# Cache attention of a decoder step: the rotary half of the scores moved from TensorE to GpSimd and VectorE

## The reference, cut to what matters

```python
def mla_keys(ckv, kpe, w_uk, g_kn):
    k_nope = jnp.einsum('btc,chd->bthd', ckv, w_uk)           # 256 latents -> 8 heads x 64
    k_pe = jnp.broadcast_to(kpe[:, :, None, :], k_nope.shape[:3] + (QK_ROPE_DIM,))   # 32, shared by the heads
    return rms_norm(jnp.concatenate([k_nope, k_pe], axis=-1), qk_gain(g_kn))

def update(carry, ckv_blk, kpe_blk, mask):                    # for every page of the cache
    k = mla_keys(ckv_blk, kpe_blk, w_uk, g_kn)
    s = jnp.einsum('bqhd,bkhd->bhqk', qf, k) * scale
    ...
```

## Time and profile before

| | |
|---|---|
| median of 3 runs | 2243.34 us (2241.21 to 2244.95) |
| span of the profiled execution | 2241.9 us; its time outside the span is not recorded, the median of the runs is 1.4 us above the span |
| cache attention within it | about 412 to 1338 us, eight sequences, 116.3 us from one tail to the next |
| TensorE busy | 2191.6 us (98%) |
| VectorE busy | 1425.7 us (64%) |
| ScalarE busy | 955.5 us (43%) |
| GpSimd busy | 363.4 us (16%) |
| granted TensorE clock, mean | 0.994 |

### The profile page before, as it was taken

One profiled execution on the slowest core, in us unless ns is written; L12 is line 12 of the kernel. 1 busy time (PEld: TensorE's weight loads), 2 busy tenths in 40 slices (PEclk: granted clock), 3 DMA queues, 4 the chain that ended last, 5 costly groups with the idle time before them and its releaser, 6 DMA issues.

```text
span 2241.9 us, 34172 instructions
## 1 busy us (share of the span) xinstructions
PE 2191.6 (98%) x12929; PEld 1845.9 (82%) x12929; DVE 1425.7 (64%) x2682; ACT 955.5 (43%) x1829; POOL 363.4 (16%) x501
## 2 busy tenths in 40 slices
PE   8999899999999999999999999999999999999999
PEld 7987566788787878787878787889999999977776
DVE  4446676576666666676767676667676767654345
ACT  4445566555454545454545463321211111133233
POOL 2554111122121313030303022100000000000000
PEclk9999999999999999999999999999999999999999
DMA  5310100242231314040405024321111111044353
GB/s 167 60 29 1 60 16 20 96 154 88 77 99 59 116 43 132 28 148 22 148 8 186 11 75 133 95 76 45 44 47 47 47 47 47 28 163 138 143 181 130
DMA packets 94628, 182.17 MB, mean 81 GB/s; under 512 B 9265, under 2 KB 64385, under 8 KB 86128
## 3 DMA queue, kind: packets, MB, share of 16 engines
q1 hardware_dynamic: 78781, 95.48, 13.3%
q0 software_dynamic: 15712, 84.92, 11.6%
HBM read 166.34 MB, written 14.35 MB: 81 GB/s over the span
## 4 chain that ended last, share of the span: by engine, by line
PE 79%; DVE 1%; ACT 1%; issue 0%; DMA 0%; POOL 0%; ACTq 0%; DVEq 0%; POOLq 0%
PE ca_banks L1702 31%; PE ca_banks L2336 22%; PE ca_banks L2609 11%; PE ca_banks L1678 5%; PE ca_banks L1783 4%; PE ca_banks L1730 3%; PE ca_banks L1718 1%; PE ca_banks L1710 1%; PE ca_banks L2585 0%; PE ca_banks L1814 0%; DVE ca_room L2447 0%; DVE ca_down_lo L2649 0%; DMA ca_w_raw<-in_w_o 0%; ACT ca_down_hi L2640 0%; PE ca_banks L1767 0%
## 5 line engine op out<-in xcount | busy, mean ns | idle before, releaser
L1974 ACT ACTIVATE ca_banks<-ca_banks 128x512 f32<-128x512 f32 x512 | 298.1, 582 | 352.4 <-PE ca_banks L1702 241.3
L1702 PE MATMUL ca_banks<-cache_w_hi,ca_hi 128*128 128x512 f32 x1024 | 424.7, 415 | 1.7 <-DVE ca_cells L2178 1.1
L1702 PE MATMUL ca_banks<-cache_w_hi,ca_lo 128*128 128x512 f32 x1024 | 401.5, 392 | 0.0
L1702 PE MATMUL ca_banks<-cache_w_lo,ca_hi 128*128 128x512 f32 x1024 | 401.2, 392 | 0.0
L2180 DVE TENSOR_REDUCE ca_cells<-ca_banks 128x8 f32<-128x512 f32 x512 | 347.9, 680 | 0.0
L1702 PEld LDWEIGHTS ca_banks<-cache_w_hi,ca_lo 128*128 128x128 f32 x1024 | 192.5, 188 | 44.8
L2065 DVE TENSOR_TENSOR ca_lo<-ca_banks,ca_hi 128x512 fp32r<-128x512 f32 x256 | 175.5, 686 | 84.6 <-ACT ca_hi L1874 76.8
L1702 PEld LDWEIGHTS ca_banks<-cache_w_hi,ca_hi 128*128 128x128 f32 x1024 | 192.7, 188 | 36.5 <-issue 1.8
L1702 PEld LDWEIGHTS ca_banks<-cache_w_lo,ca_hi 128*128 128x128 f32 x1024 | 193.3, 189 | 32.2
L2178 DVE TENSOR_TENSOR ca_cells<-ca_banks,attn_coef 128x8 f32<-128x8 f32 x512 | 84.2, 164 | 205.8 <-ACT ca_banks L1974 195.5
L1874 ACT ACTIVATE ca_hi<-ca_banks 128x512 fp32r<-128x512 f32 x256 | 152.6, 596 | 76.3 <-PE ca_banks L1678 75.1
(11 more groups left out here) (408 smaller groups left out, 4088.1 us busy)
## 6 DMA issues: line engine op xcount, KB each, us to landing
ca_down_raw<-in_w_down SPq DMA_DIRECT2D x44, 512.0 KB, 3.6
keep_w_uv<-in_w_gate SPq DMA_DIRECT2D x22, 512.0 KB, 3.9
ca_up_raw<-in_w_up SPq DMA_DIRECT2D x22, 512.0 KB, 3.7
keep_ctx<-in_w_down SPq DMA_DIRECT2D x22, 512.0 KB, 4.2
late_room<-in_x_prompt SPq DMA_DIRECT2D x8, 512.0 KB, 3.9
ca_m<-mixed_scratch SPq DMA_DIRECT2D x8, 512.0 KB, 4.0
ca_w_raw<-in_w_o SPq DMA_DIRECT2D x16, 256.0 KB, 2.7
ca_x<-in_x_prompt SPq DMA_DIRECT2D x8, 512.0 KB
```

The lines of the kernel that those rows point to most:

```text
L1702: last = nc.tensor.matmul(KK[:, t, :], x[:, n % 2, t, ck, :], w[:, par, ck, :], start=(m == 0), stop=(m == 5))
L1974: nc.scalar.activation(SQ[:, t, :], KK[:, t, :], ACT.Square).then_inc(squared, 1)
```

## The change

TensorE no longer transposes the rotary keys nor multiplies them, and ScalarE no longer copies them. For every pair of tiles GpSimd multiplies 2 x 32 rotary key numbers with the 8 x 32 rotary query numbers (512 products in each partition, `product`, first instruction), then adds the upper 16 of each 32 products to the lower 16 (256 additions, second instruction). VectorE sums the remaining 16 for each of 2 x 8 scores (128x16 from 128x256). It does so two pairs later (`PRODUCT_LAG`), and there are two product buffers, so product n waits until VectorE has read product n-2. The query numbers come in as a row that SyncE loads for each sequence from a scratch in DRAM.

GpSimd's queue is rearranged: 32 products per sequence, with the parts of the previous sequence's tail after products 1, 2, 4, 5 and 13 and the gathers of the next sequence after products 20 to 30. `mean` is computed in place of `ss`.

```diff
+MEAN_AT, RAW_AT, NORM_AT, OWN_AT, SHIFT_AT = 1, 2, 4, 5, 13
+GATHER_AT = {20: (0, 1), 22: (2,), 23: (3,), 25: (4,), 27: (5,), 28: (6,), 30: (7,)}
+PRODUCT_LAG = 2
...
+            def load_q(b):
+                sp.dma_start(q_row[b % 2], row_broadcast(keep.q_dram[b:b + 1, :], NH * DR)).then_inc(q_in[b % 2], 16)
...
+            def product(b, u):
+
+                par, k, made = b % 2, 2 * (u % 4), b * PAIRS + u
+                if u == 0:
+                    pool.wait_ge(q_in[par], 16 * (b // 2 + 1))
+                if u % 4 == 0:
+                    pool.wait_ge(slot_in[par * CHUNKS + u // 4], 32 * (b // 2 + 1))
+                if made >= 2:
+                    pool.wait_ge(product_read, made - 1)
+                keys = kpe[:, (b * CHUNKS + u // 4) % RING, k * DR:(k + 2) * DR].rearrange("p (k d) -> p k d", d=DR)
+                step(nc.gpsimd.tensor_tensor(products[u % 2][:].rearrange("p (k h) d -> p k h d", h=NH),
+                                             keys.unsqueeze(2).to_broadcast([P, 2, NH, DR]),
+                                             q_row[par].rearrange("p (h d) -> p h d", d=DR).unsqueeze(1)
+                                             .to_broadcast([P, 2, NH, DR]), ALU.mult))
+                halves = products[u % 2][:].rearrange("p t (a d) -> p t a d", a=2)
+                nc.gpsimd.tensor_tensor(halves[:, :, 0, :], halves[:, :, 0, :], halves[:, :, 1, :], ALU.add)\
+                  .then_inc(product_made, 1)
...
+            def sequence(par, b, r):
+                for n in range(PAIRS):
...
+                    product(b, n)
+                    if b >= 1:
+                        if n == MEAN_AT:
+                            tail_mean(b - 1)
+                        if n == RAW_AT:
+                            tail_raw(b - 1)
+                        if n == NORM_AT:
+                            tail_norm(b - 1)
+                        if n == OWN_AT:
+                            tail_scale(b - 1)
+                            tail_own(b - 1)
+                        if n == SHIFT_AT:
+                            tail_shift(b - 1)
+                    if b + 1 < NB and n in GATHER_AT:
...
+                        for k in GATHER_AT[n]:
+                            paced(b + 1, k)
...
-            def turn_rotary(par, b, n):
...
-            def rotary(par, b, n):
...
-                act.wait_ge(pe_turned, b * CHUNKS + n + 1)
...
-                nc.scalar.activation(kpeT[:].rearrange("p g k -> p (g k)"), KP[:, 0:2 * P], ACT.Copy).then_inc(pe_kept, 1)
...
+                    if n >= PRODUCT_LAG:
+                        rotary_scores(par, b, n - PRODUCT_LAG)
+                    elif later:
+                        rotary_scores(1 - par, b - 1, PAIRS - PRODUCT_LAG + n)
...
+            def rotary_scores(par, b, u):
+                dve.wait_ge(product_made, b * PAIRS + u + 1)
+                nc.vector.tensor_reduce(rot[:, par, 2 * u:2 * u + 2, :].rearrange("p t h -> p (t h)"), products[u % 2][:, :, 0:HR],
+                                        AX.X, ALU.add).then_inc(product_read, 1)
```

More of the change, by code:

```diff
@@ L1448, in cache_and_merge @@
         kss = cells[:, :, cut[3]:cut[4]]
-        kpeT = after("kpeT", [P, 2, P])
+        product_at = top_of[-1]
+        ctx_turned = after("ctx_turned", [P, 2, P])
+        merged = after("merged", [P, 2, P])
         squares_at = top_of[-1]
         kpe_sq = after("kpe_sq", [P, 8, DR])
-        q_pe = after("q_pe", [P, 2, P])
-        mean = after("mean", [P, TILES, NH])
+        head_rows = after("head_rows", [P, TILES, NH])
+        products = [c.at(f"product{n}", [P, 2 * NH, DR], F32, at) for n, at in enumerate((product_at, squares_at + 4 * 8 * DR))]
+        q_row = [c.at("q_row_even", [P, NH * DR], F32, small)[:], keep.q_row_odd[:]]
+        assert 4 * NH * DR <= 4 * EXTRA
         guess, tmp = (keep.w_uv[:, n, :].rearrange("p (t h) -> p t h", h=NH) for n in range(2))
@@ new lines, in tail_mean @@
+            def tail_mean(b, a=0, z=TILES):
+                mean = ss[:, b % 2, a:z]
+                if b >= 1 and a == 0:
+                    pool.wait_ge(shifted, b)
+                pool.wait_ge(summed, b * TILES + z)
+                pool.wait_ge(pe_summed, b * CHUNKS + z // 8)
+                step(nc.gpsimd.tensor_tensor(mean, mean, kss[:, b % 2, a:z].unsqueeze(2)
+                                             .to_broadcast([P, z - a, NH]), ALU.add))
+                nc.gpsimd.tensor_scalar(mean, mean, 1.0 / DH, EPS, ALU.mult, ALU.add).then_inc(averaged, 1)
@@ new lines, in tail_raw, with tail_norm @@
+            def tail_raw(b, a=0, z=TILES):
+                pool.wait_ge(scored, b * TILES + z)
+                pool.wait_ge(product_read, b * PAIRS + z // 2)
+                step(nc.gpsimd.tensor_tensor(raw[:, b % 2, a:z], raw[:, b % 2, a:z], rot[:, b % 2, a:z], ALU.add))
+            def tail_norm(b, part=0, a=0, z=TILES):
+                pool.wait_ge(averaged, b + 1 + part)
+                pool.wait_ge(guessed, b + 1 + part)
+                step(newton_rsqrt(nc.gpsimd, step, guess[:, a:z], ss[:, b % 2, a:z], guess[:, a:z], tmp[:, a:z]))
@@ L1638, in tail @@
                                         .to_broadcast([P, TILES + 1, NH]), ALU.subtract).then_inc(shifted, 1)
-            step = Steps(pool, pool_step)
-            def paced(b):
-                for n in range(CHUNKS):
-                    pool.wait_ge(summed, (b - 1) * TILES + START + PACE * n // 2)
-                    gather(nc, io, keep, b, (n,))
-            gather(nc, io, keep, 0, (1, 2))
-            for n in range(3, CHUNKS):
-                pool.wait_ge(summed, TILES // CHUNKS * (n - 2))
-                gather(nc, io, keep, 0, (n,))
@@ L1659, in _ @@
+            gather(nc, io, keep, 0, (1, 2))
+            sequences(pool, sequence)
+            chunk_sums(0)
+            b = NB - 1
+            tail_mean(b, *PARTS[1])
+            tail_raw(b, *PARTS[1])
+            tail_norm(b, 1, *PARTS[1])
+            tail_scale(b, *PARTS[1])
+            tail_own(b)
+            chunk_sums(1)
+            tail_shift(b)
             for i in range(2, NT):
@@ L1704, in keys @@
                     last.then_inc(keyed, 1)
-            def turn_rotary(par, b, n):
-                if n >= 1 or b > 0:
-                    pe.wait_ge(pe_out, b * CHUNKS + n)
-                for g in range(2):
-                    last = nc.tensor.transpose(KP[:, g * P:(g + 1) * P],
-                                               kpe[:, (b * CHUNKS + n) % RING, g * P:(g + 1) * P], keep.ident[:])
-                last.then_inc(pe_turned, 1)
-            def rotary(par, b, n):
-                pe.wait_ge(pe_kept, b * CHUNKS + n + 1)
-                for g in range(2):
-                    last = nc.tensor.matmul(KP[:, (2 + g) * P:(3 + g) * P], kpeT[:, g, :], q_pe[:, par, :],
-                                            start=True, stop=True)
-                last.then_inc(pe_scored, 1)
             def weigh(par, b):
@@ L1738, in sequence @@
                 for n in range(PAIRS):
-                    if n == 0:
-                        pe.wait_ge(q_set, b + 1)
-                    if n % 4 == 0:
-                        turn_rotary(par, b, n // 4)
+                    if n == 0 and not first:
+                        pe.wait_ge(w_set, b)
                     if n == 11 and not first:
@@ L1754, in sequence @@
                     keys(par, b, n)
-                    if n % 4 == 1:
-                        rotary(par, b, n // 4)
             def sum_squares(i):
```

139 lines of the change are left out of this document (60 added, 79 removed).

## The result

| | before | after |
|---|---|---|
| median of the runs | 2243.23 us (2241.21 to 2244.95) | **2285.53 us** (2279.94 to 2287.71) |
| the profiled execution | span 2241.9 | 2279.94, span 2278.2 |
| mean granted clock | 0.994 | 0.986 |
| one sequence | 116.2 us | 121.8 and 120.7, by turns |

The ratio is 1.0187, with a 95% interval of 1.0172 to 1.0202: the change costs 42 us, where 33 were forecast. The profiled execution of after is its fastest, so a comparison of spans shows 36.3 of the 42 us.

What follows compares the result with a forecast made beforehand. TensorE bounds the kernel before; after the change GpSimd's strict queue is late at each sequence border. Terms -39.7 (TensorE), +64.4 (borders), +4 and +4 (VectorE's waits, last sequence) give +32.7 on 2243.3: 2276 us, range 2234 to 2302.

Steps and rivals of the forecast that it cites:

- What leaves TensorE: Cache stage: rotary transposes and matmuls leaving TensorE save 0.62 us per chunk, 39.7 us in all, 5.0 per sequence.
- VectorE is not the bound: Cache stage: VectorE needs about 2.4 us of each 3.22 us pair, 3.0 in pairs 17 to 25.
- GpSimd's prices: GpSimd's products: multiplication 1.28 us, halves 0.73, two gaps of 0.08, so 2.17 us per product; gathers 2.35 per chunk.
- 9.2 us late, once per sequence: Product 20 to next sequence's mean square: GpSimd needs 53.8 us against 44.6; at seven borders 64.4 us added.
- the 44.6 us: Sequence border: time available to GpSimd from product 20 until ScalarE needs the mean square, from TensorE's 14 pairs.
- Who waits: Sequence border: VectorE waits for products from about pair 26, then ScalarE at `guess_norms`, squares queued behind, so TensorE stands.
- Rival 2, the clock: Each border: TensorE's stall drops its clock to 1.2 GHz, losing 1.7 us, +12 us in seven, 2288 us; chance 25%.
- the forecast: Whole kernel: the main case, listed as fourth among the rivals, 2265 to 2282 us; chance 45%.
- The shared reads: VectorE's two-SBUF-input instructions and GpSimd's SBUF reads exclude each other: 2.7 us in the border count, VectorE's waits 4 us.
- The sum: Whole kernel: -39.7 + 64.4 + 4 + 4 = +32.7 us, giving 2276 us on the median.
- the waits beside the splits of the output weights: Last sequence: twelve splits take VectorE to about 3.5 us per pair where 3.22 are there, 4 us.
- every sign that I had named: Profile: key matmuls idle 50 to 80 us, mean squares 120 to 122 apart, multiplication about 1.3, halves 0.73, GpSimd near 900.

Runs made afterwards that it cites:

- e4: The changed kernel with GpSimd's two product instructions cut to 64 and 32 numbers from 512 and 256, most rotary parts left out: 2209.9 us, ratio 0.9858 to before.
- e8: The changed kernel with ScalarE asking for the mean at pair 4 instead of 3, Newton step and own score one product later: 2254.9 us, ratio 1.0039 to before.
- e1: The changed kernel with GpSimd's mean square behind product 0 instead of product 1: 2257.0 us, ratio 1.0060 to before.
- e5: e4 with GpSimd's two product instructions whole again in products 16 to 24 of every sequence: 2228.05 us, ratio 0.9921 to before.

## Why the prediction was right, and where its sum was not

**What leaves TensorE** (39.7 us, 5.0 per sequence): 4.8 by e4. Right.

**VectorE is not the bound** and "a faster GpSimd would bring nearly the whole 39.7": e4 gives 34 of them, seven sequences at 4.8; the eighth is the last one with its pair 27. Right.

**GpSimd's prices.** The multiplication at 1.28 measured 1.29, the halves at 0.73 measured 0.74 where undisturbed. The count had one gap too many: a product that follows another starts as the halves end (606.86 and 608.94 in the trace), so a product costs 2.08 and not 2.17, and 14 of them 1.3 us less. From product 20 (599.49) to the end of the mean square (650.44) it is 51.0 us where I had 53.8. The shared reads took 0.65 of GpSimd's time there (two additions at 1.06 and 1.07) and not 2.7, while the gathers took 2.4 per chunk in place of 2.35.

**"9.2 us late, once per sequence" is the step that failed in size**, for these reasons and for one that I left out: the 44.6 us that TensorE was to take over the same pairs are longer, because the waits of VectorE's refresh lengthen pairs 20, 21 and 25 by 2.0. That gives GpSimd time: 51.0 - 44.6 - 2.0 would be 4.4. The pairs 0 and 3 are longer by 1.57 and 4.88 us. About 1.6 of that is the clock: from 652.91 to 656.31 eight matmul starts are 0.43 apart in place of 0.23. The stall without the clock is thus 4.9 us per border, 34 in seven, not 64.

**Who waits**: the chain was named link by link as the timeline shows it, `guess_norms` and the squares queued behind it included, and e8 shows that this link is what made it long.

**Rival 2, the clock** (25%, +12 us) came true together with the forecast; the two were never exclusive, and I priced them as if they were. 1.6 us at three borders and 2.7 at three others are 13 us. The Trainium skill (TensorE: Matmul & The Clock Gate, Part 1) ties the fall to idle time of TensorE; this trace agrees so far as it falls behind six gaps of 3.09 to 3.13 us and stays up behind one of 3.06 and behind the 1.05 us of e1. In the kernel before it fell behind a gap of 1.86 us, so the length of the gap alone doesn't decide it.

**The shared reads** (4 us for VectorE's waits): the mechanism was right, the size was wrong by five. I let only the two instructions before pair 20 count, at half a GpSimd instruction, because VectorE has least room there, and put the rest at nothing. In the trace all six cost about 0.63 more on average, the pairs 17 to 25 have no room for it, and e5 prices it at 2.35 us per sequence. The diagonal, a `tensor_scalar` on one tensor of 8 x 8 numbers and a column of 8 scalars in SBUF, was not in my count at all: 0.47 per sequence. Together 2.8 x 7 = 20 us. The Trainium skill (SBUF — State Buffer, section "Who interferes with whom") lists `tensor_scalar` among the instructions that can take the shared ports, if its operands allow it; the 0.22 us that grow to 0.84 agree. No run tells whether the tensor or the column of scalars does it here.

**The sum.** Six sequences: -4.8 + 2.8 + 4.9 + 2.1 = +5.0 us each, against 121.22 - 116.19 = 5.03 measured. The starts of the mean square, from the view of one line's instructions (count, shortest, median and longest ns, first and last start), give the same, before and after:

```profile
L1620 POOL TENSOR_TENSOR ca_mean<-ca_cells x7: 1082/1083/1086, 525.4 to 1222.6; 128x512 f32<-128x512 f32 x7
```

```profile
L1649 POOL TENSOR_TENSOR ca_cells<-ca_cells x7: 1073/1074/1080, 526.9 to 1254.2; 128x512 f32<-128x512 f32 x7
```

The distance from first to last grows from 697.2 to 727.3 us: 30 us in six sequences. The rest is worked out from TensorE's rows in the two traces. From its first key matmul to the end of sequence 0 the changed kernel takes 3.1 us less, in the last sequence 9.6 more, and behind the last key matmul 4.6 more. That makes 41 of the 42 us. (The profiled execution reaches the first key matmul 4.9 us earlier than that of before; in those of the ten experiments this start lies anywhere from 408.8 to 415.2 us, so I count it as scatter.)

The last sequence has its border (4.9, with the clock up), the waits beside the splits of the output weights (3.1 us in pairs 20, 22 and 24, for which I had 4), and the stall in pair 27, 4.9 us longer than before, which my count of seven borders did not contain. Behind the last key matmul TensorE waits 2.6 us for GpSimd's sum of squares (L1619), which stands behind the last products, and the clock falls again for 3.4 us; I had no term for that stretch either.

So the direction, the chain and the seven borders were right, and every sign that I had named came true (idle time of 51.4 us, 121.2 us between mean squares, 1.29 and 0.74 us, GpSimd busy for 890). That the time was met within 10 us is luck: a border term too large by 30 (64 for 34) stood in for the clock (0 for 13), VectorE's waits (4 for 20) and some 10 us at the end of the stage and behind it that had no term.

## What to carry to other kernels

Work given to GpSimd has a second price that its own idle time doesn't show: a VectorE instruction with two SBUF inputs, and here a small `tensor_scalar` too, waits until GpSimd's instruction is done (0.68 us became 1.27 to 1.36 on average), so list those instructions first and move them (here onto GpSimd itself, 2.4 us per sequence) or put them beside gathers, well before the next product: one that began in the last 0.5 us of a gather waited for the whole product behind it. An engine with a strict queue must be costed over the stretch where its work is dense, not over the sequence; and where it is late, look at which in-order engine asks for its result ahead of work that others need, for asking one pair later was worth as much (31 us) as any saving. The change itself was sound: with the refresh and the diagonal off VectorE, the halves no longer added on GpSimd, the gathers spread and the mean asked for later, it gives 2218.5 us, 1.2% below the kernel before. Its pair 27 of the last sequence still takes 9.3 us where the kernel before needs 4.1.
